# Finer dependency keys for one buffer in a self-scheduling kernel: each head's write to `ktT` gets a key of its own

## The reference, cut to what matters

```
rq, rk, rv, rg, hq, hf, hi, hg = split(rmsnorm(x) @ w_in)
# retention: rotary on rq, rk; decay gamma_h; o = (q k^T * decay) v + q S;  S <- S*decay + k^T v
# HGRN2:     hq = silu(hq) * 128**-0.5
f     = lb + (1 - lb) * sigmoid(hf)
log_f = log(f);  k_in = 1 - f;  v_in = hi
b     = cumsum(log_f) in a chunk
A     = (q * exp(b)) @ (k_in * exp(-b))^T, causal;   o = A v + (q * exp(b)) S
o     = head_rmsnorm(o) * silu(gate);   x = x + concat(o_ret, o_hgrn) @ w_out
x     = x + square(relu(rmsnorm(x) @ w_up)) @ w_down;   y = rmsnorm(x)
```

## Time and profile before

| | |
|---|---|
| median of 3 runs | 1297.53 us (1297.48 to 1300.32) |
| the profiled execution | 1299.48 us |
| its span on the slowest core, core 3 | 1297.9 us |
| spans of the eight cores | 1276.8 to 1297.9 us |
| PE, DVE, ACT, POOL busy | 77%, 35%, 36%, 27% of the span |

### The profile page before, as it was taken

One profiled execution on the slowest core, in us unless ns is written; L12 is line 12 of the kernel. 1 busy time (PEld: TensorE's weight loads), 2 busy tenths in 40 slices (PEclk: granted clock), 3 DMA queues, 4 the chain that ended last, 5 costly groups with the idle time before them and its releaser, 6 DMA issues.

```text
span 1297.9 us, 20447 instructions; the slowest of 8 cores (1276.8 to 1297.9 us)
## 1 busy us (share of the span) xinstructions
PE 997.0 (77%) x5972; PEld 521.0 (40%) x5973; DVE 458.5 (35%) x807; ACT 472.7 (36%) x821; POOL 346.5 (27%) x349
## 2 busy tenths in 40 slices
PE   0748055777879889874536996999999999979986
PEld 0335033244545445543222442444454444434432
DVE  0423043646667666558982100030130130040003
ACT  2337035254567556546521332041231232142301
POOL 1220111432233233236520242043032123203500
PEclk9869576787889979796567998999999999999988
DMA  9889999930000100005669243367456465533233
GB/s 215 117 152 106 103 113 114 123 68 3 17 31 18 33 2 1 1 1 158 193 171 335 102 130 130 131 209 283 157 175 256 155 220 203 195 131 114 98 130 130
DMA packets 60381, 163.02 MB, mean 126 GB/s; under 512 B 3312, under 2 KB 29040, under 8 KB 49776
## 3 DMA queue, kind: packets, MB, share of 16 engines
q1 hardware_dynamic: 42528, 134.45, 30.4%
q0 software_dynamic: 17744, 27.26, 17.4%
HBM read 171.13 MB, written 36.70 MB: 160 GB/s over the span
## 4 chain that ended last, share of the span: by engine, by line
PE 53%; DMA 19%; DVE 9%; issue 8%; ACT 7%; another core or an unknown queue 2%; POOL 1%; DVEq 0%; ACTq 0%; SPq 0%; POOLq 0%
PE ps L553 51%; DMA arena<-w_in 7%; ACT arena L566 6%; DVE arena L574 4%; DMA wu_s<-w_up 4%; DVE arena L585 3%; DMA wo_s<-w_out 3%; DMA wd_s<-w_down 3%; PE ps L557 2%; ACT L566 2%; DMA arena<-wd_s 1%; DMA arena<-x 1%; DMA arena<-wu_s 1%; POOL arena L574 1%
## 5 line engine op out<-in xcount | busy, mean ns | idle before, releaser
L553 PE MATMUL ps<-arena 128*128 128x512 bf16 (+4 forms) x5360 | 965.5, 334 | 209.1 <-DVE arena L574 100.2
L553 PEld LDWEIGHTS ps<-arena 128*128 128x128 bf16 (+2 forms) x5360 | 483.3, 104 | 664.5 <-issue 326.1
L574 POOL TENSOR_TENSOR arena<-arena 128x384 bf16<-128x384 f32 (+4 forms) x318 | 325.9, 1045 | 711.3 <-ACT arena L566 463.1
L566 ACT ACTIVATE arena<-ps 128x512 f32<-128x512 f32 (+4 forms) x347 | 200.8, 608 | 441.1 <-PE ps L553 335.2
L574 DVE TENSOR_TENSOR arena<-arena,ps 128x512 f32<-128x512 f32 x148 | 98.7, 682 | 529.1 <-PE ps L553 456.6
L566 ACT ACTIVATE arena<-arena 128x1024 bf16<-128x1024 f32 (+6 forms) x336 | 166.9, 516 | 246.3 <-DVE arena L574 190.5
L566 ACT ACT_TABLE_LOAD x87 | 111.6, 1283 | 132.3 <-DVE arena L585 67.8
L585 DVE SCALAR_TENSOR_TENSOR arena<-arena 128x128 bf16<-128x128 f32 (+3 forms) x136 | 111.0, 829 | 118.3 <-ACT arena L566 116.4
L557 PE MATMUL ps<-arena 128*128 128x128 bf16 x612 | 89.4, 246 | 80.0 <-DVE arena L585 51.1
L574 DVE TENSOR_TENSOR arena<-ps,arena 128x256 f32<-128x256 f32 (+1 forms) x187 | 85.1, 487 | 57.4 <-PE ps L553 39.0
L557 PEld LDWEIGHTS ps<-arena 128*128 128x128 bf16 x612 | 54.5, 110 | 100.0 <-issue 95.7
(11 more groups left out here) (9 smaller groups left out, 5.3 us busy)
## 6 DMA issues: line engine op xcount, KB each, us to landing
arena<-wu_s SPq DMA_DIRECT2D x40, 1024.0 KB, 5.8
arena<-wd_s SPq DMA_DIRECT2D x40, 1024.0 KB, 5.7
arena<-x SPq DMA_DIRECT2D x34, 512.0 KB, 8.6
y<-arena SPq DMA_DIRECT2D x17, 512.0 KB, 3.0
arena<-w_in POOLq DMA_DIRECT2D x4, 2048.0 KB, 20.5
wu_s<-w_up POOLq DMA_DIRECT2D x8, 1024.0 KB, 47.9
wd_s<-w_down POOLq DMA_DIRECT2D x8, 1024.0 KB, 37.1
srs<-arena SPq DMA_DIRECT2D x4, 1024.0 KB, 6.0
```

Of the source, the lines that this page charges most:

```text
L553: S.compute("pe", lambda e: e.matmul(RZ(out), lhsT=lhsT, rhs=rhs, start=start, stop=stop), r, w, cost=0.036 + fsz(rhs) * 0.00039)
L566: return e.activation(out=RZ(out), in_=RZ(in_), func=func, scale=scale, **kw)
L574: S.compute(eng, lambda e: e.tensor_tensor(out=RZ(out), in0=RZ(in0), in1=RZ(in1), op=op), r, w, cost=ecost(eng, out))
```

## The change

The key of each of the four writes to `ktT` becomes `("PART", K("ktT"), h)`. A partial write depends on the last whole write, on the last write of the same part, on all readers of the whole buffer, and on readers of that part. A reader of the whole buffer (the transposes and the `ktT` by `qtT` matmuls still name the whole) depends on the last writers of all parts. So the four writes no longer depend on each other, and the wait of each on the one before is gone; each of PE's readers still waits for all four. Nothing that is computed changes, and no instruction is added or removed.

```diff
         for r in reads:
-            w = self.last_writer.get(r)
-            if w is not None:
-                deps.add(w)
+            if is_part(r):
...
+            else:
+                w = self.last_writer.get(r)
+                if w is not None:
+                    deps.add(w)
+                for w in self.part_writer.get(r, {}).values():
+                    deps.add(w)
         for w_ in writes:
...
+            if is_part(w_):
+                base, part = w_[1], w_[2]
+                w = self.last_writer.get(base)
+                if w is not None:
+                    deps.add(w)
+                w = self.part_writer.get(base, {}).get(part)
+                if w is not None:
+                    deps.add(w)
+                for rd in self.readers.get(base, ()):
+                    deps.add(rd)
+                for rd in self.part_readers.get(base, {}).get(part, ()):
+                    deps.add(rd)
...
               for h in range(4):
                   STT(ktT[:, h, :], B3h[:, h, :], homl[:, h:h + 1], B2h[:, h, :], ALU.mult, ALU.mult,
-                      [K("B3"), K("B2"), "homl"], [K("ktT")])
+                      [K("B3"), K("B2"), "homl"], [("PART", K("ktT"), h)])
```

More of the change, by code:

```diff
@@ L37, in __init__ @@
         self.readers = {}
+        self.part_writer = {}
+        self.part_readers = {}
         self.n_dma_sems = n_dma_sems
@@ L69, in _add, with is_part @@
         deps = set()
+        def is_part(k_):
+            return isinstance(k_, tuple) and len(k_) == 3 and k_[0] == "PART"
         for r in reads:
-            w = self.last_writer.get(r)
-            if w is not None:
-                deps.add(w)
-        for w_ in writes:
-            w = self.last_writer.get(w_)
-            if w is not None:
-                deps.add(w)
-            for rd in self.readers.get(w_, ()):
-                deps.add(rd)
+            if is_part(r):
+                base, part = r[1], r[2]
+                w = self.last_writer.get(base)
[10 more added lines that the diff above has]
+                    deps.add(w)
+        for w_ in writes:
+            if is_part(w_):
+                base, part = w_[1], w_[2]
+                w = self.last_writer.get(base)
+                if w is not None:
+                    deps.add(w)
+                w = self.part_writer.get(base, {}).get(part)
+                if w is not None:
+                    deps.add(w)
+                for rd in self.readers.get(base, ()):
+                    deps.add(rd)
+                for rd in self.part_readers.get(base, {}).get(part, ()):
+                    deps.add(rd)
+            else:
+                w = self.last_writer.get(w_)
+                if w is not None:
+                    deps.add(w)
+                for w in self.part_writer.get(w_, {}).values():
+                    deps.add(w)
+                for rd in self.readers.get(w_, ()):
+                    deps.add(rd)
+                for lst in self.part_readers.get(w_, {}).values():
+                    for rd in lst:
+                        deps.add(rd)
         deps.discard(op.id)
@@ L82, in _add @@
         for r in reads:
-            self.readers.setdefault(r, []).append(op.id)
+            if is_part(r):
+                self.part_readers.setdefault(r[1], {}).setdefault(r[2], []).append(op.id)
+            else:
+                self.readers.setdefault(r, []).append(op.id)
         for w_ in writes:
-            self.last_writer[w_] = op.id
-            self.readers[w_] = []
+            if is_part(w_):
+                self.part_writer.setdefault(w_[1], {})[w_[2]] = op.id
+                self.part_readers.setdefault(w_[1], {})[w_[2]] = []
+            else:
+                self.last_writer[w_] = op.id
+                self.readers[w_] = []
+                self.part_writer[w_] = {}
+                self.part_readers[w_] = {}
         self.ops.append(op)
```

## The result

The changed kernel takes 1277.69 us, median of 10 runs (1274.64 to 1388.07); the kernel before, run beside it on the same chip, 1297.64 us (10 runs). The ratio is 0.9851, with a 95% interval of 0.9829 to 0.9872. Some runs of most kernels fall into a slower state of one die; ratios and profiles here leave them out. The forecast was 5 us faster; it is 20 us faster, and lies 3 us outside the range.

The account below looks back on a forecast made before the run. Bounds taken: DMA up to 257 us, PE in stretch A, DVE in B and C; segment 1, PE-busy, untouched. 6.5 - 1 - 6 - 4.5 = -5.0 us off the 1297.53 us median gave 1292.5 us, range 1281 to 1304.

Parts of the forecast that it names:

- The last cast unchanged: DMA-bound stretch up to 257 us: POOL's last weight cast still starts at 256.36 us.
- The waits worth 1 us: DVE's removed waits on itself between ktT writes, stretch A: 1 us of gain, ends 0 and 7.8 us.
- Stretch A: 257 to 583 us, last cast to release of w_in: 34 more PE rows, +6.5 us, and -1 us for waits.
- No row tells what they become: Stretch A: the 56 us in which PE waited, taken as unchanged, 11 us either way.
- the price of a row: Stretch A: busy PE per row, 0.278 us for 128x512 and 0.115 us for 128x128, giving +6.5 us.
- The 11 us either way: Range for PE's waits in stretch A, from its two halves differing by 5.7 us of idle PE.
- Stretch B: 583 to 643 us, to T16's last ktT row: eleven DVE rows less on the pace-setting engine, -6 us.
- Stretch C: 643 to 685 us, four sample heads on DVE: 6.1 us of Vexp loss gone, +1.6 us other rows, -4.5 us.
- Segment 1 as long as before: The program from 685 us on: not touched by the change, 613 us as before.
- The path through the tiles gets shorter too: Rival, stretch A: ktT reaches PE earlier, 7.8 us gained instead of 1, -11.8 us, 1285.7 us; chance 0.20.
- Slower, by `Vexp`: Rival, 583 to 685 us: POOL's Vexp rows stall more of DVE, up to +10.4 us on the forecast, 1303; chance 0.22.
- Nothing left: Rival, stretch B: a chain sets it, not DVE's sum, so -6 falls away, +1 us, 1298.5; chance 0.20.

Follow-up runs that it names:

- e1: Order of the kernel before, only the 51 waits of DVE on itself between the ktT writes removed: 1302.55 us, ratio 0.9988 to the kernel before.
- e2: Order of the changed kernel, but each ktT write waits again for the one before it: ratio 0.9910 to the kernel before.
- n1: Kernel before, its order kept, all table functions of segment 0 replaced by Identity (other values, no table loads there): 1275.31 us, ratio 0.9784.
- n2: Changed kernel, its order kept, all table functions of segment 0 replaced by Identity (other values): 1266.17 us, ratio 0.9722 to the kernel before.
- e3: Kernel before, ktT writes still dependent on each other, but list-schedule priorities computed as if they weren't: ratio 0.9929 to the kernel before.
- e4: Changed kernel, ktT writes independent, but list-schedule priorities computed with the old chain: ratio 0.9992 to the kernel before.
- w1: Kernel before with a list-schedule rule against table loads (ACT prefers rows of the present table, loads planned at 2.6 us): 1294.81 us, ratio 0.9940.
- w2: Changed kernel with a list-schedule rule against table loads (ACT prefers rows of the present table): 1268.76 us, ratio 0.9736 to the kernel before.
- x1: Changed kernel with the list-schedule rule against table loads in segment 0 alone: 1263.87 us, ratio 0.9709 to the kernel before.

## Why the prediction was right or wrong, step by step

**The last cast unchanged: right.** 256.4 and 257.1 us on the slowest cores.

**The waits worth 1 us, between 0 and 7.8: right for the old order, too low for the new.** The 0.19 us for one wait was right (0.58 us for three), and e1 gained nothing that can be told. But "The order before already put another row into nearly every gap" is a reading of the order that the change replaces: in the new one the four rows stand together in 12 of 17 tiles, and e2 against the changed kernel says 8 us (3 to 13). PE's waits for those rows are no measure of it; in A of the slowest core they grew.

**Stretch A, +6.5 - 1 us: wrong, and nearly the whole miss.** The median core shows PE busy for 3.2 us less and waiting for 5.8 us less: 8.7 us shorter instead of 5.5 longer. The count was not at fault: 29 rows more on the slowest cores where 34 were forecast (of 837 rows that could stand ahead of the cast only 829 did, so 5 moved in from there and not 13), which is about 1 us. Two steps failed. The first is "No row tells what they become", said of the 56 us in which PE waits. Rows did tell part of it: 14.8 us of these waits were for ACT, and 5.7% of the chain was table loads, whose number and place are set by the order that changes. The earlier trace rows gave ACT's share of the stretch (185 of 326 us); its share of the chain was not asked for. The second is the price of a row, taken as fixed. n1 and n2 show both: without loads the forecast's terms come out at +6.7 and -1.9. With them the old order pays 13.7 us of waiting and 15.3 us of busy PE for its loads (56.4 - 42.7, 271.1 - 255.8), the new one 9.8 and 5.4. The difference, 3.9 + 9.9 = 13.8 us, is the miss of 14.2. With e1 and e2 in the place of before and after it is 15.0 and 11.9 against 14.3 and 1.5 us, 11 us in all, nearly all of it in busy PE: that the loads make the miss holds, how it parts is less firm.

The price moves in good part because TensorE's clock does: 271.1 us at a mean clock of 0.870 are 235.9 us of full clock, 255.8 at 0.905 are 231.5, so some 10 of the 15.3 us are clock, by this estimate. Windows of 4 us of the kernel before, around one of its waits (for DVE, with no load near):

```profile
290.00:294.00 4.00, 1.43 (x7) 0.71 (x8) 4.00 (x11) 0.52 (x2) 1.42 (x2) 1.00 0.15 59
294.00:298.00 4.00, 1.89 (x23) 1.23 (x20) 3.76 (x11) 0.50 (x2) 1.32 (x2) 1.00 0.00 0
298.00:302.00 4.00, 1.30 (x9) 0.66 (x7) 3.90 (x10) 0.00 (x0) 1.98 (x3) 0.56 0.01 2
302.00:306.00 4.00, 4.00 (x30) 2.94 (x29) 3.10 (x8) 1.88 (x2) 0.24 (x1) 0.50 0.02 4
306.00:310.00 4.00, 4.00 (x48) 3.78 (x46) 1.16 (x2) 0.60 (x1) 3.64 (x4) 0.66 0.00 0
310.00:314.00 4.00, 4.00 (x37) 2.44 (x34) 0.43 (x1) 1.48 (x2) 0.00 (x0) 1.00 0.02 4
```

PE is busy 4.6 of 12 us; then the granted clock is 0.50, that is 1.2 GHz, while PE is full from 302 us on, and 2.4 GHz again at 310. A wait is paid once as a wait and again in the rows behind it. This one is there in n1 too. Not so the one behind the three loads of the chain shown above. Before, and the same rows in n1 (slowest cores):

```profile
520.00:524.00 4.00, 1.70 (x29) 1.41 (x27) 2.75 (x4) 3.94 (x6) 0.76 (x2) 0.97 0.00 0
524.00:528.00 4.00, 3.87 (x20) 2.15 (x21) 3.88 (x8) 2.43 (x4) 2.04 (x2) 0.61 0.00 0
```

```profile
504.00:508.00 4.00, 3.09 (x50) 2.75 (x49) 2.92 (x5) 2.93 (x5) 1.46 (x2) 1.00 0.00 0
508.00:512.00 4.00, 3.89 (x18) 1.68 (x18) 4.00 (x11) 0.76 (x2) 1.36 (x1) 1.00 0.00 0
```

From the same group of 26 PE rows (515.83 and 500.38 us) to the same group of 12 (522.23 and 505.36) it is 6.40 us before and 4.98 in n1: 1.42 us more, with the load ahead of the gate's Ln. Then the clock falls to 0.61 before and stays at 1.00 in n1.

**The 11 us either way: too narrow.** It came from two halves of one order. Six orders of the same rows were run here (before, after, e3, e4, w1, w2), each also without loads: with them A goes from 298 to 334 us, without from 290 to 321.

**Stretch B, -6: right.** 6.6 us less on the median core, DVE busy 43.97 us in 63 rows where it was 53.75 in 75. No DVE row there takes 5 us; the scan fell from 4.99 to 2.90, which the forecast had not counted. The four `ktT` rows stand together, but at 0.54 us each and not in 1.1 us, with POOL at work beside them. n1 and n2 differ by 8.2 us in B, so it does not hang on loads.

**Stretch C, -4.5: right, with one part off.** 4.0 us less. The transposes at 634.23 us wait for nothing. The multiplication met a `Vexp` again, the second, which ends at 643.91; it took 4.60 us, 2.3 of them lost, where the forecast had it free of loss and 1.6 us of other rows on top.

**Segment 1 as long as before: right** (608.0 and 608.5 us).

**The rivals.** "The path through the tiles gets shorter too" named the direction, at 1285.7 us, but its reason, shorter waits of PE for `ktT`, is not seen: the waits for `ktT` and `og` grew on the slowest core. That the waits on DVE were worth 7.8 us is, by e2, possible. "Slower, by `Vexp`" is refuted: the eight copies lost 5.5 us where they had lost 10.5. "Nothing left" is refuted by B.

**What stays open.** Why the new keys' order has its loads off the path is not derived from the keys, and e4 shows that the chain's share does not price them. Nor is it shown where the 8 us between e2 and the changed kernel lie. e3 and e4 each have half of the new rule and lie on both sides of before in A. The likelier reading, not shown as such, is that A is one draw from a spread of some 30 us that any change of the list schedule draws anew, while B and C are a gain that could be read from the order.

## What to carry to other kernels

Where a change lets a list schedule draw a new order, read what the chain of waits is made of on every engine, the state changes of ScalarE among them, before counting rows: an order that moves some of them off the chain can be worth more than the rows it moves (13.4 us less for loads here, against 4.7 us more without them). Price a wait by where it stands in the new order, not in the old one. Give a stretch that is reordered throughout a range as wide as orders of the same work differ, not as halves of one order do. And if any order is a draw, draw more: a rule of eight lines in the schedule (x1) was worth about as much again as the change itself (0.9709 against 0.9851).

## What the runs showed of the hardware that was not expected

A switch of tables costs 1283 ns and little more. ACT before, with starts and lengths:

```profile
515.42 1.08 ACT L566 ACTIVATE arena<-ps 128x512 f32<-128x512 f32 x2
516.62 1.28 ACT L566 ACT_TABLE_LOAD   x1
517.92 2.25 ACT L566 ACTIVATE arena<-arena 128x128 f32<-128x128 f32 x4
```

The rows before end at 516.50, the load starts 0.12 us later, and the next row 0.02 us behind it: 1.42 us in all. The Trainium skill ("ScalarE: Activation LUTs", section "What ACT_TABLE_LOAD costs") gives the same 1283 ns and adds a drain of about 1380 ns for each switch; this trace doesn't show the drain. The 53 loads in stretch A are 68.0 us of ACT and were worth 27.8 us of A, about half of it as slower rows of PE, most of that by TensorE's clock (0.870 with the loads, 0.905 without).
